# Another order of work in the mixed layers of a small float32 network: units of the projection, heads, linear attention and output projection

## The chip, the core and the metric

One core of a Trainium2 chip runs the whole network in one launch. Its engines are TensorE (PE, matrix products), VectorE (DVE), ScalarE (ACT), GpSimd (POOL) and the queue SP, which issues the loads. Each engine takes its instructions strictly in the order in which the program gives them, and waits at semaphores that the others raise. The metric is the device time of one execution in microseconds (us), lower is better.

## What is computed

The input is 256 tokens of width 1024. A first block has two layers of feed-forward (width 2816), a mixer, and feed-forward again; a second block has four layers of another kind. The change is in the mixer of the first block (called a mixed layer here), of which the core of the reference is:

```python
proj = h @ mix_w_in[l]
a_q, a_k, a_v, b_u, c_q, c_k, c_v, c_r, c_g = jnp.split(proj, splits, axis=-1)
qa = _rope(_rmsnorm(_split_heads(a_q, ATT_HEADS), q_norm[l]), cos, sin)
ka = _rope(_rmsnorm(_split_heads(a_k, ATT_HEADS), k_norm[l]), cos, sin)
o_a = _merge_heads(_moba_attention(qa, ka, va))
o_b = _conformer_conv(b_u, conv_w[l], conv_b[l], conv_norm_g[l], conv_norm_b[l])
log_decay = jax.nn.log_sigmoid(c_g @ gla_gate_w[l] + gla_gate_b[l]) / GLA_TAU
o_c = _gla(...)
o_c = _merge_heads(_rmsnorm(o_c, gla_out_norm[l])) * jax.nn.silu(c_r)
mixed = jnp.concatenate([o_a, o_b, o_c], axis=-1) @ mix_w_out[l]
x = x + gt2[:, None, :] * mixed
```

With 256 tokens the attention is one causal block: eight heads of width 64. The convolution is depthwise, 31 taps on 256 channels, then a layer norm over groups of 64 channels and swish. The linear attention has four heads of width 64. The second block's layers are differential attention (twice), HGRN (once) and a gated unit (once), each followed by cross-attention and feed-forward. All is float32 in value.

## The kernel before

**Products of split weights.** Every weight arrives as float32 in `raw`, four slots of 1 MB (a *unit*: 1024 rows by 256 columns). ACT rounds it into `whi` (line 782), DVE subtracts to get `wlo` (line 1204), and PE takes three products (high by high, high by low, low by high) into a PSUM bank. `ahead(pos)` (split_ahead) on ACT and on DVE makes these splits for units up to three ahead of `pos`, and each split waits until PE has used up the unit that held the slot before. A unit is 48 products of 256 columns, two accumulation halves of 24 products, each of which shows as two or one records in the trace.

**The mixed layer, `mix1`.** Each engine's list is written out by hand. PE (lines 2204 to 2291): thirteen units in the order c_r, c_g (half a unit), c_k, c_q, conv_a, conv_g, mq, mq, mk, mk, c_v, mv, mv; among them a small gate product, four sums of squares for the head norms (`group_sum`, line 2183) and four rope products (line 2300). Then, when all units are done, a loop of eleven steps: `scores` of head j (lines 2266 and 2267, into bank 4 or 0 by turns), transposes of head j-2 (`turn_probs`, line 1956, bank 6), `values` of head j-3 (`over_tokens`, lines 2202 and 2203, bank 7 or 3), the linear attention's three levels (lines 2243 and 2247) at j below 3, its token product at j = 4, and two sums for the convolution's norm (lines 2286 and 2290). DVE (to line 1751) copies c_v and mv out, does the 62 tap instructions (lines 1579 and 1582) in blocks of 4, 10 and 12 between the splits, the ropes, and for each head mask, maxima, reciprocal and the two scalings of the probabilities (lines 1706 to 1717). ACT copies the other units out, does roots (lines 938 and 940), the exponentials (line 945), the copies of the transposes (line 992) and the high parts of the results (line 998).

**The output projection, `outp`** (line 2505 on), is four units of the same kind (line 2518), each over eight tiles k of the mixed result; unit 0 waits tile by tile for the result's low part: tiles 0 to 3 are attention, 4 and 5 convolution, 6 and 7 linear attention. DVE adds each unit to x (line 1474), and the norm of the next feed-forward begins with squares on ACT, a sum on PE (line 2091), a logarithm and an exponential on ACT (lines 841 and 843), and then eight high and low parts (lines 856 and 1369) that release the first unit of the feed-forward tile by tile.

**HGRN** has its own list: `HGRN_ORDER`, five whole units, then levels of its recurrence between halves of units (`level`, line 2197 on PE; `up`, lines 1527 to 1540, and `keep_level`, lines 1557 and 1561 on DVE). `half(u, src, m)` is one accumulation half of a unit; the differential layer uses it to put each head between two halves.

## Time and profile before

| | |
|---|---|
| Time, median of 3 runs | 2830.16 us (2827.55 to 2834.45) |
| The profiled execution's own time | 2832.67 us |
| Its span, first to last instruction | 2830.8 us |
| Mean granted TensorE clock | 0.972 |
| PE busy in the span | 2699.1 us (95%) |
| DVE / ACT busy | 1870.0 us (66%) / 1343.5 us (47%) |
| First mixed layer, first unit to last product of the output projection | 286.3 to 446.1 us |
| Second mixed layer | 847.9 to 1008.9 us |

The times are of one profiled execution. A busy share is an average over stages. Where lines of PE stand as x2, two records were merged; matmuls are pipelined, so that the start of the next instruction less the start of this one is what an instruction costs in a full queue, and the printed duration is longer. PEclk is the granted clock as a share of 2.4 GHz: 0.50 is 1.2 GHz.

### The profile page before, as it was taken

What the parts mean: (1) busy time and instruction counts of PE and PEld (TensorE: products, weight loads), DVE (VectorE), ACT (ScalarE), POOL (GpSimd) and SP (SyncE); (2) the same over time, 40 slices, a digit from 0 to 9 for tenths busy, and PEclk for the clock granted to TensorE, in tenths of its full rate; (3) what the DMA queues carried; (4) which work ended last, traced back from release to release, by engine and by line L of the source; (5) the groups of instructions that cost most, each with busy time, mean ns of one, the idle gap of its engine ahead of it and who ended that gap; (6) DMA issues with size and microseconds to landing.
All of it is one profiled execution on the core that took longest, in us unless ns stands there. A gap on an engine that the chain in (4) does not pass through costs nothing.

```text
span 2830.8 us, 52843 instructions
## 1 busy us (share of the span) xinstructions
PE 2699.1 (95%) x22247; PEld 2615.9 (92%) x22247; DVE 1870.0 (66%) x2575; ACT 1343.5 (47%) x1578; POOL 3.5 (0%) x7
## 2 busy tenths in 40 slices
PE   6799979999999799999999999999999999999998
PEld 5799859999999499999999999999999999999998
DVE  5788776887877655576565666656565555775564
ACT  3334634435445354455544535544455544655443
POOL 0000000000000000000000000000000000000000
PEclk8899979999999699999999999999999999999999
DMA  8988505997985046654355643535665365643553
GB/s 234 310 291 273 179 30 187 300 294 263 299 282 164 30 150 200 205 189 162 101 199 179 210 147 105 164 135 196 220 194 179 105 208 198 209 145 118 179 192 105
DMA packets 458801, 533.05 MB, mean 188 GB/s; under 512 B 9880, under 2 KB 435082, under 8 KB 458634
## 3 DMA queue, kind: packets, MB, share of 16 engines
q1 hardware_dynamic: 457340, 530.11, 57.4%
q8 instruction: 112, 1.84, 0.3%
q10 hardware_dynamic: 1293, 0.65, 0.1%
q14 instruction: 56, 0.45, 0.0%
HBM read 528.10 MB, written 2.62 MB: 187 GB/s over the span
## 4 chain that ended last, share of the span: by engine, by line
PE 84%; DVE 8%; ACT 3%; issue 2%; DMA 2%; SPq 1%; ACTq 0%; DVEq 0%
PE ps L2134 15%; PE ps L1965 12%; PE ps L1966 12%; PE ps L1967 12%; PE ps L1983 10%; PE ps L2518 8%; DVE wlo L1204 2%; DMA work<-in_ada_w 2%; PE ps L2168 2%; DVE work L1582 1%; PE ps L2327 1%; PE ps L2329 1%; PE ps L2328 1%; PE ps L2091 1%; DVE work L1308 1%
## 5 line engine op out<-in xcount | busy, mean ns | idle before, releaser
L1204 DVE TENSOR_TENSOR wlo<-raw,whi 128x2048 fp32r<-128x2048 f32 (+1 forms) x514 | 975.8, 1918 | 411.5 <-ACT whi L782 411.3
L782 ACT ACTIVATE whi<-raw 128x2048 fp32r<-128x2048 f32 (+1 forms) x514 | 827.7, 1616 | 442.3 <-PE ps L1967 181.6
L1965 PE MATMUL ps<-hhi,whi 128*128 128x256 f32 x1600 | 451.9, 282 | 16.0 <-issue 14.2
L1966 PE MATMUL ps<-hlo,whi 128*128 128x256 f32 x1600 | 445.5, 278 | 0.0
L1967 PE MATMUL ps<-hhi,wlo 128*128 128x256 f32 x1600 | 445.1, 278 | 0.0
L1965 PE MATMUL ps<-parts_f,whi 128*128 128x256 f32 x1344 | 372.9, 277 | 8.0 <-issue 8.0
L1966 PE MATMUL ps<-parts_f,whi 128*128 128x256 f32 x1344 | 371.8, 277 | 0.0
L1967 PE MATMUL ps<-parts_f,wlo 128*128 128x256 f32 x1344 | 371.5, 276 | 0.0
L2134 PE MATMUL ps<-ghi,whi 128*128 128x256 f32 x1280 | 355.5, 278 | 7.9 <-DVE wlo L1204 7.9
L2134 PE MATMUL ps<-glo,whi 128*128 128x256 f32 x1280 | 355.5, 278 | 0.0
L2134 PE MATMUL ps<-ghi,wlo 128*128 128x256 f32 x1280 | 355.2, 278 | 0.0
L1965 PEld LDWEIGHTS ps<-hhi,whi 128*128 128x128 f32 x1600 | 303.7, 190 | 20.3 <-issue 20.3
L1966 PEld LDWEIGHTS ps<-hlo,whi 128*128 128x128 f32 x1600 | 303.8, 190 | 0.7 <-issue 0.7
L1967 PEld LDWEIGHTS ps<-hhi,wlo 128*128 128x128 f32 x1600 | 303.4, 190 | 0.0
L1965 PEld LDWEIGHTS ps<-parts_f,whi 128*128 128x128 f32 x1344 | 252.3, 188 | 9.5 <-issue 9.4
L1966 PEld LDWEIGHTS ps<-parts_f,whi 128*128 128x128 f32 x1344 | 252.3, 188 | 0.1
L1967 PEld LDWEIGHTS ps<-parts_f,wlo 128*128 128x128 f32 x1344 | 252.3, 188 | 0.0
L2134 PEld LDWEIGHTS ps<-ghi,whi 128*128 128x128 f32 x1280 | 241.5, 189 | 8.6 <-issue 8.6
L2134 PEld LDWEIGHTS ps<-glo,whi 128*128 128x128 f32 x1280 | 241.5, 189 | 0.0
L2134 PEld LDWEIGHTS ps<-ghi,wlo 128*128 128x128 f32 x1280 | 241.4, 189 | 0.0
L1308 DVE SCALAR_TENSOR_TENSOR work<-work,silu_c 128x256 f32<-128x256 f32 x490 | 196.9, 477 | 0.0
L1983 PE MATMUL ps<-hhi,whi 128*128 128x256 f32 x880 | 177.9, 284 | 16.3 <-DVE hlo L1369 16.3
(299 smaller groups left out, 4818.2 us busy)
## 6 DMA issues: line engine op xcount, KB each, us to landing
raw<-in_ffn_w_in SPq DMA_DIRECT2D x88, 1024.0 KB, 10.5
raw<-in_ffn_w_gu SPq DMA_DIRECT2D x88, 1024.0 KB, 5.1
work<-in_ada_w SPq DMA_DIRECT2D x72, 1024.0 KB, 8.9
raw<-in_ffn_w_out SPq DMA_DIRECT2D x88, 512.0 KB, 5.9
raw<-in_ffn_w_down SPq DMA_DIRECT2D x88, 512.0 KB, 5.5
raw<-in_ca_w_kv SPq DMA_DIRECT2D x32, 1024.0 KB, 5.6
raw<-in_mix_w_in SPq DMA_DIRECT2D x24, 1024.0 KB, 6.2
raw<-in_da_w_in SPq DMA_DIRECT2D x24, 1024.0 KB, 5.5
```

What stands on the lines that cost most here:

```text
L782: f(whi[:, s, 0:size], raw[:, s, 0:size], ACT.Copy).then_inc(hi_done[s], 1)
L1204: tt(wlo[:, s, 0:size], raw[:, s, 0:size], whi[:, s, 0:size].bitcast(F32), ALU.subtract).then_inc(lo_done[s], 1)
L1308: m = stt(acc, w, silu_c[:, k:k + 1], acc, ALU.mult, ALU.add)
L1582: m = stt(conv_acc[:, t, :], h, w, conv_acc[:, t, :], ALU.mult, ALU.add)
L1965: mm(dst, wh, xh, start=first, stop=False)
L1966: mm(dst, wh, xl, start=False, stop=False)
L1967: return mm(dst, wl, xh, start=False, stop=last)
L1983: o = mm(ps[:, slot, 256 * m:256 * m + 256], w[:, k, P * m:P * m + P], x_[:, k, :], start=k == 0 and i == 0 and m == 0, stop=k == KT - 1 a ...
L2091: o = mm(ps[:, st.bank, 0:S], ones, norm_x[:, k, :], start=k == 0, stop=k == KT - 1)
L2134: o = mm(dst, a_, b_[:, t, :], start=first and t == 0 and i == 0 and m % 2 == 0, stop=False, skip_group_check=True)
L2168: o = mm(dst, a_, b_[:, t, :], start=False, stop=t == 1 and i == 2 and m % 2 == 1, skip_group_check=True)
L2518: o = mm(ps[:, bank, 256 * m:256 * m + 256], w[:, k, P * m:P * m + P], x_[:, k, :], start=k == 0 and i == 0 and m == 0, stop=k == KT - 1 a ...
```

## The change

In the mixed layer the thirteen units come in the order of `MIX_ORDER`: convolution's gate and input first, the gate of linear attention, then queries and keys by turns, and the rest; their PSUM banks go round over three. From the fourth unit on PE takes each unit in halves, and head norms, ropes, scores, transposes, values and the levels of linear attention stand between halves. Scores now use bank 4 alone, values bank 7 alone, sums bank 5, ropes bank 3. Masking, maxima and reciprocal stay on DVE; the scaling of probabilities, and the copying out of mv and c_v, move to ACT. DVE's taps lie in blocks of 2 to 10 over the whole layer, 15 or more at its end. Two merged predicated copies take the place of four in the linear attention's `keep`. The output projection is taken in parts (`out(n, *ks)`), by the tiles that are ready: 0 and 1 of its units among the last heads, then 2, 3, 6 and 7, and last 4 and 5; the order 0, 1, 2, 3, 6, 7, 4, 5 is in `ORDER`. Its inputs lie in `fhi`/`flo` in place of `hhi`/`hlo`; `outp` on PE does nothing after a mixed layer, and during it ACT and DVE call `ahead` for two of its units only, DVE after the last addition to x. In the HGRN layer `hf` comes ahead of `hq`, and DVE's `ahead(us[LEAD].pos)` moves from before the first level's `keep` to after it.

```diff
                       ("dk", 1, 2), ("dv", 2, 2), ("dq", 0, 3), ("dk", 1, 3), ("dv", 2, 3))
+        MIX_ORDER = (("conv_g", 1792, 0, 256), ("conv_a", 1536, 0, 256), ("c_g", 2960, 0, P), ("mq", 0, 0, 256),
+                     ("mk", 512, 0, 256), ("mq", 0, 1, 256), ("mk", 512, 1, 256), ("mv", 1024, 0, 256),
+                     ("c_k", 2304, 0, 256), ("c_q", 2048, 0, 256), ("mv", 1024, 1, 256), ("c_v", 2560, 0, 256),
+                     ("c_r", 2816, 0, 256))
         LEAD = 5
-        HGRN_ORDER = (("hq", 0, 0), ("hq", 0, 1), ("hf", 1, 0), ("hf", 1, 1), ("hq", 0, 2),
+        HGRN_ORDER = (("hf", 1, 0), ("hf", 1, 1), ("hq", 0, 0), ("hq", 0, 1), ("hq", 0, 2),
                       ("hq", 0, 3), ("hf", 1, 2), ("hf", 1, 3), ("hv", 2, 0), ("hv", 2, 1), ("hv", 2, 2),
                       ("hv", 2, 3), ("hgate", 3, 0), ("hgate", 3, 1), ("hgate", 3, 2), ("hxv", 4, 0),
...
-        def out_project(w, mod=None):
-            units = plan.columns(w, 0, 4, "out")
+        def out_project(w, mod=None, banks=None):
+            units = [plan.column(w, 0, "out", n, banks[n] if banks else plan.slot) for n in range(4)]
...
-            units += plan.columns(w, 1024, 2, "mv", token_major=True)
+            units = [plan.column(w, c0, name, i, n % 3, token_major=name in ("mv", "c_v"), cols=cols, bank=name not in ("mq", "mk"))
+                     for n, (name, c0, i, cols) in enumerate(MIX_ORDER)]
...
+                                masked=take("masked", 8), pairs=take("pairs", 4), rope=take("rope", 4),
+                                reads=list(plan.reads)))
...
+            ready = out_project(a["mix_w_out"][l], mod=(l, 1), banks=(1, 2, 0, 3))
+            mixed.out = stages[-1]
...
+                def probabilities(j):
+                    s, r = m_s[:, j % 2, :], stat[:, j % 2]
+                    act.wait_ge(q["scaled"], st.heads + j + 1)
+                    f(s[:, 0:P], s[:, 0:P], ACT.Copy, scale=r[:, 8:9])
+                    f(s[:, P:384], s[:, P:384], ACT.Copy, scale=r[:, 9:10]).then_inc(q["probs"], 1)
...
+                tt(conv_h[:, :, CONV_K - 1:], rows2(ps[:, us[1].b, :]), conv_sig, ALU.mult).then_inc(read[us[1].b], 1)
+                dve.wait_ge(*bank_read(us[1]))
+                taps_on(4)
+                ahead(us[2].pos)
+                taps_on(4)
+                gate_least()
+                ahead(us[3].pos)
+                taps_on(2)
+                gate_sums()
+                ahead(us[4].pos)
+                taps_on(3)
+                normed(0)
+                taps_on(6)
+                ahead(us[5].pos)
+                normed(1)
+                rope(0)
+                taps_on(4)
+                ahead(us[6].pos)
+                normed(2)
+                rope(1)
+                ahead(us[7].pos)
+                maxima(0)
+                normed(3)
+                rope(2)
+                inverse(0)
+                maxima(1)
+                ahead(us[8].pos)
+                inverse(1)
+                maxima(2)
                 rope(3)
-                causal = const("causal")
-                for j in range(8 + 3):
-                    if j < 8:
...
+                maxima(4)
+                queries_in()
+                inverse(4)
+                ahead(us[10].pos)
+                maxima(5)
+                taps_on(2)
+                inverse(5)
+                keep(0)
+                low(1)
+                ahead(us[11].pos)
+                maxima(6)
+                taps_on(2)
+                inverse(6)
+                keep(1)
+                far()
+                maxima(7)
+                taps_on(2)
+                inverse(7)
+                ahead(us[12].pos)
+                keep(2)
+                low(2)
+                taps_on(10)
+                ahead(st.out.units[0].pos)
+                taps_on(8)
+                low(3)
+                taps_on(2 * CONV_K)
...
+                tt(rows2(m_t[:, 0, :]), rows2(m_t[:, 0, :]), c_r, ALU.mult).then_inc(q["gla_out"], 1)
+                dve.wait_ge(q["conv_mm"], 2 * l + 1)
+                dve.wait_ge(q["taps_v"], base + 2 * CONV_K)
+                stt(conv_acc, rows2(ps[:, 4, :]), -1.0 / HD, conv_acc, ALU.mult, ALU.add).then_inc(q["conv_v"], 1)
                 dve.wait_ge(q["gla_hi"], l + 1)
                 dve.wait_ge(q["gla_out"], l + 1)
-                tt(hlo[:, 6:8, :], rows2(m_t[:, 0, :]), hhi[:, 6:8, :].bitcast(F32), ALU.subtract)\
+                tt(flo[:, 6:8, :], rows2(m_t[:, 0, :]), fhi[:, 6:8, :].bitcast(F32), ALU.subtract)\
...
@@ -1854,7 +1949,7 @@
                         for m in range(H_DONE[g - 1], H_DONE[g]):
                             evict(us[m + 1])
                             ahead(us[m + 2].pos)
-                    else:
+                    if g == 1:
                         ahead(us[LEAD].pos)
                     if g == LEVELS + 5:
                         normed(0)
...
+                def values(h):
+                    pair = h // 2
+                    pe.wait_ge(q["turned"], st.heads + h + 1)
+                    pe.wait_ge(*bank_read(us[7 if h < 4 else 10]))
+                    if h == 0:
+                        pe.wait_ge(q["gate_v"], 2 * l + 1)
+                        pe.wait_ge(q["gate_s"], 3 * l + 1)
+                    if st.pairs + pair > 0:
+                        pe.wait_ge(q["values_lo"], st.pairs + pair)
+                    over_tokens(ps[HD * (h % 2):HD * (h % 2) + HD, 7, 0:S], mv, slice(HD * h, HD * h + HD),
+                                m_pt[:, h % 2, :]).then_inc(q["values_mm"], 1)
...
+                def conv_sum(n):
+                    if n == 0:
                         pe.wait_ge(q["taps_v"], 2 * CONV_K * (l + 1))
...
+                        pe.wait_ge(q["masked"], st.masked + 8)
+                    else:
...
+                def out(n, *ks):
+                    u = outs[n]
...
+                    if ks[0] == ORDER[0]:
+                        weights(u)
+                        if u.read > 0:
+                            pe.wait_ge(read[u.b], u.read)
+                    th, tl = tiles(u.slot)
+                    bank = out_bank(st.out, n)
+                    for k in ks:
+                        pe.wait_ge(*mixer_tile(st.out, k))
+                        for i, (w, x_) in enumerate(((th, fhi), (th, flo), (tl, fhi))):
+                            for m in range(2):
+                                o = mm(ps[:, bank, 256 * m:256 * m + 256], w[:, k, P * m:P * m + P], x_[:, k, :],
+                                       start=k == ORDER[0] and i == 0 and m == 0,
+                                       stop=k == ORDER[-1] and i == 2 and m == 1, skip_group_check=True)
+                    if ks[-1] == ORDER[-1]:
+                        o.then_inc(used[u.slot], 1)
+                for n in range(3):
+                    unit(us[n], "h", st.h)
+                half(us[3], "h", 0)
+                gates()
+                half(us[3], "h", 1)
+                half(us[4], "h", 0)
+                head_sum(0)
+                half(us[4], "h", 1)
+                half(us[5], "h", 0)
+                head_sum(1)
...
+                half(us[5], "h", 1)
+                pe.wait_ge(q["gn_out"], st.gn + 1)
+                half(us[6], "h", 0)
+                head_sum(2)
+                rope(1)
+                half(us[6], "h", 1)
+                pe.wait_ge(q["gn_out"], st.gn + 2)
+                half(us[7], "h", 0)
+                head_sum(3)
+                rope(2)
+                scores(0)
+                half(us[7], "h", 1)
+                scores(1)
+                pe.wait_ge(q["gn_out"], st.gn + 3)
+                half(us[8], "h", 0)
+                rope(3)
+                turn_head(0)
+                scores(2)
+                half(us[8], "h", 1)
+                turn_head(1)
+                values(0)
+                pe.wait_ge(q["gn_out"], st.gn + 4)
+                half(us[9], "h", 0)
+                turn_head(2)
+                values(1)
+                scores(3)
+                half(us[9], "h", 1)
+                scores(4)
+                half(us[10], "h", 0)
+                values(2)
+                turn_head(3)
+                scores(5)
+                half(us[10], "h", 1)
+                turn_head(4)
+                values(3)
+                gla_level(0)
+                half(us[11], "h", 0)
+                turn_head(5)
+                scores(6)
+                half(us[11], "h", 1)
+                values(4)
+                gla_level(1)
+                half(us[12], "h", 0)
+                values(5)
+                turn_head(6)
+                scores(7)
+                half(us[12], "h", 1)
+                gla_level(2)
+                out(0, 0, 1)
+                values(6)
+                turn_head(7)
+                out(1, 0, 1)
+                gla_tokens()
+                out(2, 0, 1)
+                values(7)
+                out(0, 2)
+                out(1, 2)
+                group_sum(st.gn + 4, 3, m_sq, block)
+                out(2, 2)
+                conv_sum(0)
+                out(0, 3)
+                out(1, 3)
+                out(2, 3)
+                out(3, 0, 1)
+                conv_sum(1)
+                out(3, 2, 3)
+                for n in range(4):
+                    out(n, 6, 7)
+                for n in range(4):
+                    out(n, 4, 5)
...
             def outp(st):
+                if st.mixer.kind == "mix1":
+                    return
```

## Rows read from the trace of the kernel before

**Rows 1.** The page, section 1: busy time of each engine over the whole span
```profile
PE 2699.1 (95%) x22247; PEld 2615.9 (92%) x22247; DVE 1870.0 (66%) x2575; ACT 1343.5 (47%) x1578; POOL 3.5 (0%) x7
```

**Rows 2.** Busy time by stretch (columns in its first line), first mixed layer
```profile
core 0: us, PE busy (x) PEld busy (x) DVE busy (x) ACT busy (x) POOL busy (x), PEclk, DMA share, GB/s
286.30:376.00 89.70, 79.36 (x622) 73.82 (x623) 72.80 (x108) 47.04 (x47) 1.39 (x1) 0.97 0.49 155
376.00:420.00 44.00, 37.69 (x150) 22.72 (x149) 26.08 (x83) 16.34 (x50) 0.00 (x0) 0.60 0.00 1
420.00:446.10 26.10, 24.12 (x195) 23.86 (x194) 13.21 (x17) 13.10 (x14) 0.00 (x0) 0.93 0.34 116
```

**Rows 3.** The same view: a differential layer, HGRN's levels, after a norm
```profile
1209.40:1341.80 132.40, 131.33 (x1090) 125.15 (x1089) 91.95 (x123) 76.84 (x128) 0.00 (x0) 1.00 0.52 167
...
1650.00:1700.00 50.00, 45.39 (x377) 44.84 (x375) 35.15 (x60) 15.81 (x14) 0.00 (x0) 0.97 0.33 106
...
452.00:458.00 6.00, 5.68 (x35) 5.71 (x36) 5.41 (x14) 4.02 (x8) 0.00 (x0) 0.72 0.00 0
```

**Rows 4.** The chain that ended last, in time: start, us, what
```profile
286.34 6.32 PE ps L1983 x48
...
446.05 3.47 PE ps L2091 x16
...
452.32 7.35 PE ps L1983 x48
...
847.93 7.40 PE ps L1983 x48
...
1008.88 3.47 PE ps L2091 x16
...
1353.83 21.80 PE ps L1983 x192
```

**Rows 5.** Timeline of PE, small matmuls: start, us, engine, line, operation, shape
```profile
399.81 0.55 PE L1956 MATMUL ps<-con,work 128*128 128x128 f32 x3
...
400.29 0.65 PE L2202 MATMUL ps<-work 128*64 128x256 f32 x2
...
401.09 0.48 PE L2266 MATMUL ps<-work 64*128 64x128 f32 x2
...
407.51 1.91 PE L2183 MATMUL ps<-work,con 128*128 128x512 f32 x2
...
409.35 0.79 PE L2266 MATMUL ps<-work 64*128 64x128 f32 x2
```

**Rows 6.** Timeline of DVE: taps, weight split, rope, one head's maxima
```profile
340.80 4.83 DVE L1582 SCALAR_TENSOR_TENSOR work<-work,taps 128x256 f32<-128x256 f32 x12
...
345.54 2.29 DVE L1204 TENSOR_TENSOR wlo<-raw,whi 128x2048 fp32r<-128x2048 f32 x1
...
348.41 0.68 DVE L1594 TENSOR_TENSOR work<-ps,cs 128x512 f32<-128x512 f32 x1
...
350.33 4.83 DVE L1582 SCALAR_TENSOR_TENSOR work<-work,taps 128x256 f32<-128x256 f32 x12
...
387.07 0.55 DVE L1706 TENSOR_TENSOR work<-ps,con 128x384 f32<-128x384 f32 x1
...
388.18 0.15 DVE L1518 RECIPROCAL stat<-stat 128x2 f32<-128x2 f32 x1
```

**Rows 7.** Timeline of ACT: a table load; the last weight split before a norm; ACT free after it
```profile
319.29 1.28 ACT L820 ACT_TABLE_LOAD   x1
...
435.26 1.92 ACT L782 ACTIVATE whi<-raw 128x2048 fp32r<-128x2048 f32 x1 [3.52 <-PE ps L2518]
...
457.09 1.28 ACT L873 ACT_TABLE_LOAD   x1
```

**Rows 8.** Timeline at HGRN's first two levels: DVE, then PE
```profile
1640.85 2.29 DVE L1204 TENSOR_TENSOR wlo<-raw,whi 128x2048 fp32r<-128x2048 f32 x1 [2.71 <-ACT whi L782]
...
1644.33 2.05 PE L2197 MATMUL ps<-work 128*128 128x128 f32 x16 [1.48 <-DVE work L1527]
```

486 lines of the change are left out of this document (238 added, 248 removed).

## Prediction

> **What bounds the kernel now.** I read the page first, then busy time by stretch, then the timeline of each engine in the stretch that stood out. The page says PE is busy for 95% of the span [rows 1], which looks like a kernel with nothing to gain from order. That is an average. By stretch [rows 2], the first mixed layer has three parts: 89.7 us of units (clock 0.97), 44.0 us in which the heads, linear attention and convolution's norm run alone, and 26.1 us of output projection. In the middle part PE counts as busy for 37.7 us, but at a granted clock of 0.60, so that its work is 37.7 x 0.60 = 22.6 us at full clock; DVE is busy for 26.1 us of the 44 and ACT for 16.3. Nobody is full: the engines hand each other one head at a time. What the layer costs from its first unit to the norm's sum is 446.05 - 286.34 = 159.7 us, and for the second layer 1008.88 - 847.93 = 161.0 us [rows 4]. The differential layer, in which heads already stand between halves of units, is the model of the other state: PE busy 131.3 of 132.4 us, clock 1.00 [rows 3].
>
> **PE's floor in the new order.** The products stay the same; only the time at which they run changes. A unit costs 21.80 / 4 = 5.45 us when the queue is full [rows 4]. Units: 12.5 x 5.45 = 68.1 us, plus 0.9 because the first is released tile by tile (6.32) [rows 4]. Output projection: 4 x 5.45 = 21.8. Small products: a sum or rope over 512 columns takes 409.35 - 407.51 = 1.84 at half clock, 0.92 at full [rows 5]; four sums, four ropes and the gate product (512 columns too) that now lie among the units are 9 x 0.92 = 8.3, and with the 22.6 from above 30.9. Floor: 68.1 + 0.9 + 21.8 + 30.9 = 121.7 us a layer. Of the 30.9 the heads take most: transposes 400.29 - 399.81 = 0.48, values 401.09 - 400.29 = 0.80, scores (as many columns) the same, so 8 x 2.08 = 16.6 [rows 5].
>
> **DVE in the new order.** It is busy for 72.8 + 26.1 + 13.2 = 112.1 us of the layer [rows 2]. Sixteen scalings and three copies go to ACT (an estimate of 7 us: 0.3 each for the scalings, 0.64 for a copy, a third of the rope's three passes over as many elements), about 105 us stay, less than PE's floor, so DVE isn't the bound by its sum; what matters is where its work lies. Its prices from start to start: twelve taps 345.54 - 340.80 = 4.74, so 0.395 each; a rope's three passes 350.33 - 348.41 = 1.92; a weight split 2.2; mask and maxima 388.18 - 387.07 = 1.1 [rows 6]. Followed down the three lists, DVE keeps ahead of PE through the early units, since each unit gives it 5.45 us against a split of 2.2 and 1 to 3 us of taps or ropes. The weak place is the end. PE issues `scores(7)` after 11.5 units' worth plus a half, 65.4, the 0.9, and 30.9 - 6.8 of small products (6.8 for two values 1.6, one transpose 0.5, level and tokens some 1.9, three sums 2.8): 90.4, with a little handshake 91. From there DVE has, without a gap: mask and maxima 1.1, two taps 0.8, the reciprocal 0.3, a split 2.2, `keep` 0.9, `low` 0.35, ten taps 3.95, a split 2.2, eight taps 3.2, `low` 0.35, and the last 62 - 47 = 15 taps 5.9. That is 21.3, so the taps end at 112.3. `conv_sum(0)` waits for them in PE's queue, and PE reaches it at about 91 + 2.7 (half unit) + 5.0 (small) + 6.1 (nine tiles of output, 0.68 each) = 105. PE therefore idles for 7 us there, and all the remaining output parts stand behind that wait although their tiles may be ready. After it: 0.9 + three tiles 2.0 + two 1.4 + sum 0.9 + two 1.4 + eight 5.4 + eight 5.4 = 17.5 (rounded from tiles of 0.68), end at 129.8. The convolution's own chain from 113.2 (mean 0.7, square 0.6, PE's sum at its turn ending 117.5, root 1.3, gain 0.8, table 1.3 [rows 7] and swish 0.9, high 0.6, low 0.7) is ready at 123.1, and PE needs it at 124.3: hidden by only 1.2 us, and one for one on the path beyond that.
>
> **Clock.** After the norm's wait PE starts at half clock, 0.72 over six us [rows 3], and its first unit takes 7.35 where 6.32 was seen [rows 4]. I charge the 7 us wait at `conv_sum(0)` the same 1.0. First layer 131, second layer 132 (it starts at 7.40 [rows 4]). Saved: 159.7 - 131 = 28.7 and 161.0 - 132 = 29.0, together 57.7.
>
> **What is lost behind the layer.** Now the second unit of the following feed-forward is rounded by ACT at 435.26, while the output projection runs [rows 7]. In the change `outp` calls `ahead` for two units only, so this split moves behind the norm's last high part: ACT is free at 457.09 [rows 7], rounds in 1.9, DVE subtracts in 2.2, ready at 461.3. PE is through with the first unit at 452.32 + 7.35 = 459.7 [rows 4]. That is 1.6 us of idle a layer, 3.2 in all; queued behind are all products of the feed-forward. The first unit's `wlo`, which DVE does after its last addition to x, lies beside square, sum and root (the first product comes 6.3 us after the sum starts [rows 4]) and costs nothing. Loads cost nothing: the DMA share is 0.49, 0.00 and 0.34 in the three stretches [rows 2], and the same 17 MB in 131 us is about 130 GB/s.
>
> **HGRN.** DVE waits 2.71 us for ACT's rounding before it can do the second level's factor, and PE idles 1.48 for it [rows 8]. The moved `ahead` takes this wait out of the way; the work that comes next in DVE's list has slack of a half unit. With `hf` first, its DVE part is done before `hq` is there, which PE isn't waiting for today. I take 1.5; bounds 0 and 3.5 (the wait could return at the next level, or a second one of the same sort could go too).
>
> **Other edits.** Merged `keep` copies the same elements in half as many instructions, within 0.5 us. The half unit c_g moves from second to third place, so that DVE splits a whole unit before the norm's scaling: 1 us more, inside its wait for the root; if that cover were gone, 1 us a layer. ACT does about 5 us more scaling and 2 of copies; it is busy 76 of 160 us [rows 2].
>
> **Sum.** 57.7 - 3.2 + 1.5 = 56.0. Against the profiled execution (2832.67 us, span 2830.8) this gives 2776.7. The median of the runs is 2.5 below that execution: 2774.
>
> **Rivals.** *Floor* (0.10): DVE is faster than I lay out or PE slower early, so that the taps are done when PE comes; 122.7 and 123.7 a layer, with the upper HGRN value 37.0 + 37.3 + 3.5 - 0 = 77.8, so 2752. For it: the differential layer idles only 1.1 us [rows 3]. Against: that layer has no taps.
> *Handshakes* (0.12): a head's round trip is scores 0.8, maxima 1.1, exponentials 1, scaling 0.9, transposes 0.5, copy 0.5, values 0.8, and with a DVE split of 2.2 and an ACT split of 1.9 in between nearly 10 us, against some 8 us between heads with only two in flight and now one bank for scores. If each of eight costs PE 1.5 more, the layer takes 143 and the time is 2798. Against: in the differential layer the same trip hides.
> *Slower, by the clock* (0.05): the change puts a wait into nearly every half unit. Now the long units run clear of heads at 0.97 while only the small products suffer at 0.60 [rows 2]; if the small waits pull the clock down among the units too, the last 4.5 units, the 4 of output (8.5 x 5.45 = 46) and 15 us of small products run at 1.2 GHz: 192 a layer, 2893 in all. It decides where more than 29 us of a layer's work falls to half clock. Against it: from 1650 to 1700 PE has such waits (busy 45.4 of 50) and keeps 0.97 [rows 3]. The Trainium skill has a rule for this case, speaking against the change: "TensorE: Matmul & The Clock Gate", section "A second HAM failure mode: psum-queue depth-cycling", says that many short idle gaps between groups of matmuls can make the clock oscillate. By that rule the time would be this rival's; the row of the HGRN levels bears it out hardly at all.
> *No overlap* (0.03): the chain of taps, norm and swish plus late heads eats what the interleaving gives, 2826 to 2835; DVE would have to idle 50 us a layer, which no stretch of its lists suggests.
>
> **Chances and range.** Forecast 0.70 (2757 to 2792: tail idle 3 to 12 us a layer, waits of heads up to 5). A measurement of this kernel tells about 0.3% from no change. Faster by more than that 0.92 (forecast, floor, handshakes), within it 0.03, slower 0.05. The range, 2755 to 2799, takes in handshakes and nearly the floor.
>
> **What would show it.** PE idle at the product that answers to line 2286 (sum over taps), released by DVE's taps: 5 to 9 us; clock 0.95 or more from the first head to there; a layer of 129 to 134 us; the feed-forward's second unit waiting 1 to 2 us for `wlo`; no 1.48 us wait at HGRN's second level. The prediction is wrong if transposes or values wait over 1 us for most heads, if the clock falls between units, or if ACT's splits come late because exponentials stand in front of them.

## The result, and the profile after

The changed kernel takes 2790.17 us (median of 4 runs, 2786.83 to 2792.43) against 2830.52 us before (median of 4, 2827.55 to 2834.45): a ratio of 0.9856, 95% interval 0.9839 to 0.9873. The forecast was 2774 us, range 2755 to 2799. The profiled execution took 2786.83 us with a span of 2785.0 us, where the kernel before had 2832.67 and 2830.8. It is these 45.8 us of span that the account below divides up; the medians are 40.4 us apart, since the profiled execution before lies 2.1 us above its median and the one after 3.3 us below.

Busy time of the engines over the whole span, after, and then the first mixed layer by stretch (start and end, length, busy us and instructions of each engine, granted clock, DMA share, GB/s):

```profile
PE 2675.4 (96%) x22247; PEld 2602.8 (93%) x22247; DVE 1858.3 (67%) x2525; ACT 1356.7 (49%) x1615; POOL 3.5 (0%) x7
```

```profile
284.30:300.00 15.70, 15.67 (x125) 15.70 (x126) 14.15 (x28) 11.70 (x13) 0.00 (x0) 0.90 0.58 179
300.00:384.00 84.00, 84.00 (x626) 72.32 (x625) 63.19 (x103) 51.25 (x94) 1.38 (x1) 1.00 0.42 137
384.00:402.00 18.00, 11.61 (x78) 8.82 (x76) 17.79 (x40) 6.91 (x9) 0.00 (x0) 0.94 0.00 1
402.00:419.60 17.60, 17.60 (x142) 16.63 (x140) 5.58 (x11) 10.51 (x13) 0.00 (x0) 0.96 0.00 1
```

The 44 us at clock 0.60 [rows 2] are gone. PE is busy for all of the 84 us in which heads stand between halves of units, at full clock. One hole is left, 384 to 402, and in it DVE is full (17.79 of 18.00). What PE waited for in this layer (for what, us in total, times, longest):

```profile
PE ps L2398 <- DVE work L1637: 5.8, 1, 5.8
PE ps L2078 <- DVE hlo L1422: 2.8, 1, 2.8
PE ps L2297 <- DVE parts_f L1757: 0.6, 1, 0.6
```

L2398 is `conv_sum`, L1637 a tap of the convolution; the 2.8 us are the norm's, and were there before. The chain of waits in the same layer, in order of time (start, us, what):

```profile
284.33 12.63 PE ps L2078 x96
...
379.22 0.57 DVE work L1746
...
394.50 5.21 DVE work L1637 x14
...
400.49 2.08 PE ps L2398 x2
402.56 3.92 PE ps L2415 x30
...
407.34 12.28 PE ps L2415 x108
419.62 3.67 PE ps L2186 x16
```

From the first product to the norm's sum the layer takes 419.62 - 284.33 = 135.3 us, and the second 961.86 - 825.62 = 136.2 us, where they took 159.7 and 161.0 [rows 4]. The reader should see the last taps end at 400.4 and `conv_sum` start at once.

**Where the 45.8 us are.** I took the start of every norm's sum in both traces and subtracted stretch by stretch. Mixed layers, from their first product: 24.4 + 24.8 = 49.2 gained. The feed-forward behind each layer, sum to sum, grew: 198.5 to 202.0 and 194.0 to 197.4, so 6.9 lost. The stretch with HGRN's levels went from 194.7 to 192.9, 1.9 gained. All before the first mixed layer is 2.0 shorter, though no instruction there changed, and 0.4 is lost in small amounts elsewhere. That is scatter: over all runs below, the first mixed layer begins anywhere between 282.7 and 287.1. 49.2 - 6.9 + 1.9 + 2.0 - 0.4 = 45.8.

The loss behind the layer shows in the second layer's feed-forward. Timeline of ACT, DVE and PE at its start (start, us, engine, line, operation, shape, idle before and for whom):

```profile
973.00 1.90 ACT L788 ACTIVATE whi<-raw 128x2048 fp32r<-128x2048 f32 x1
...
974.93 2.29 DVE L1257 TENSOR_TENSOR wlo<-raw,whi 128x2048 fp32r<-128x2048 f32 x1 [1.32 <-ACT whi L788]
...
977.33 0.55 PE L2060 MATMUL ps<-hhi,whi 128*128 128x256 f32 x1 [2.66 <-issue]
977.67 0.42 PE L2061 MATMUL ps<-hlo,whi 128*128 128x256 f32 x1
```

ACT rounds the second weight unit after the norm's last high part, DVE subtracts, and PE starts 0.1 us after DVE ends. The row says "issue", but DVE's end at 977.22 shows what was waited for. Behind the idle time the products come to stand 0.21 apart (0.34 for the first) instead of 0.11: half clock.

The first layer's feed-forward has something more. It streams the modulation weights of the layers to come, and here ACT's waits for its weights' loads, from the norm's sum on, are 8.6 us before (first row) and 40.6 us after (second row):

```profile
ACT whi L782 <- DMA raw<-in_ffn_w_in: 8.6, 9, 1.5
```

```profile
ACT whi L788 <- DMA raw<-in_ffn_w_in: 40.6, 19, 6.6
```

The stretches say why. Before, the last 12 us of the output projection, the 15 us behind them, and the rest of the feed-forward:

```profile
434.10:446.10 12.00, 12.00 (x107) 11.98 (x106) 4.06 (x6) 5.00 (x5) 0.00 (x0) 1.00 0.73 251
446.10:461.10 15.00, 12.18 (x79) 11.47 (x78) 7.53 (x19) 8.16 (x14) 0.00 (x0) 0.89 0.18 58
461.10:644.60 183.50, 183.26 (x1606) 183.06 (x1605) 149.41 (x235) 79.03 (x69) 0.00 (x0) 1.00 0.89 288
```

And after, the same three, with the third cut in two:

```profile
407.60:419.60 12.00, 12.00 (x107) 11.87 (x106) 4.20 (x9) 9.14 (x11) 0.00 (x0) 1.00 0.00 1
419.60:434.60 15.00, 11.04 (x65) 10.11 (x64) 11.67 (x21) 10.14 (x17) 0.00 (x0) 0.89 0.21 70
434.60:449.60 15.00, 14.28 (x123) 14.15 (x124) 8.52 (x7) 6.69 (x6) 0.00 (x0) 1.00 0.95 319
449.60:621.60 172.00, 171.41 (x1496) 171.12 (x1495) 140.99 (x228) 72.37 (x62) 0.00 (x0) 1.00 0.91 293
```

Before, the loads ran at 251 GB/s while the output projection was still on (251 x 12 = 3.0 MB); after, at 1 GB/s. A load can start when DVE has subtracted the unit that lay in its raw slot. Before, DVE does that between the additions to x, and the next load goes out 11.8 us ahead of the norm's sum (first row: the queue, start, us, loads). After, DVE comes to it behind the last addition, and the load goes out 3.3 us behind the sum, as soon as this subtraction ends (second and third row):

```profile
434.14 5.82 SPq L664 DMA_DIRECT2D raw<-in_ffn_w_in  x2
...
420.45 2.28 DVE L1257 TENSOR_TENSOR wlo<-raw,whi 128x2048 fp32r<-128x2048 f32 x1
422.81 12.62 SPq L670 DMA_DIRECT2D raw<-in_ffn_w_in  x2
```

Two things in the change could make the load late: in the parts by ready tiles all four units are used up together at the end, and ACT and DVE call `ahead` for two units only, DVE after the last addition. The run with the output projection whole (below) parts them. The feed-forward then asks for some 290 GB/s to its end and doesn't catch up.

### The profile page after: what moved, and what is told of

Read it like the earlier page. It is cut to its first block, busy times and chain, and to the rows that moved or that the text cites. A ratio compares the mean times of both kernels' runs of the same rounds, so it can differ in the third digit from the quotient of the medians.

```text
span 2785.0 us, 52844 instructions
## 1 busy us (share of the span) xinstructions
PE 2675.4 (96%) x22247; PEld 2602.8 (93%) x22247; DVE 1858.3 (67%) x2525; ACT 1356.7 (49%) x1615; POOL 3.5 (0%) x7
## 4 chain that ended last, share of the span: by engine, by line
PE 88%; DVE 5%; issue 2%; DMA 2%; ACT 2%; SPq 1%; ACTq 0%; DVEq 0%
PE ps L2229 15%; PE ps L2060 13%; PE ps L2061 13%; PE ps L2062 13%; PE ps L2078 8%; PE ps L2720 6%; PE ps L2527 2%; PE ps L2529 2%; PE ps L2528 2%; DMA work<-in_ada_w 2%; PE ps L2263 2%; PE ps L2186 1%; PE ps L2415 1%; DVE work L1361 1%; PE ps L2051 1%
## 5 line engine op out<-in xcount | busy, mean ns | idle before, releaser
L2060 PE MATMUL ps<-hhi,whi 128*128 128x256 f32 x1824 | 518.5, 284 | 21.7 <-issue 19.7
L2061 PE MATMUL ps<-hlo,whi 128*128 128x256 f32 x1824 | 508.5, 279 | 0.0
L2062 PE MATMUL ps<-hhi,wlo 128*128 128x256 f32 x1824 | 507.6, 278 | 0.0
L2060 PEld LDWEIGHTS ps<-hhi,whi 128*128 128x128 f32 x1824 | 346.4, 190 | 31.7 <-issue 31.5
L2061 PEld LDWEIGHTS ps<-hlo,whi 128*128 128x128 f32 x1824 | 346.3, 190 | 2.2 <-issue 2.2
L2062 PEld LDWEIGHTS ps<-hhi,wlo 128*128 128x128 f32 x1824 | 346.1, 190 | 0.0
L2078 PE MATMUL ps<-hhi,whi 128*128 128x256 f32 x656 | 132.3, 284 | 16.2 <-DVE hlo L1422 16.2
```

What stands on the lines that cost most here:

```text
L2060: mm(dst, wh, xh, start=first, stop=False)
L2061: mm(dst, wh, xl, start=False, stop=False)
L2062: return mm(dst, wl, xh, start=False, stop=last)
L2078: o = mm(ps[:, slot, 256 * m:256 * m + 256], w[:, k, P * m:P * m + P], x_[:, k, :], start=k == 0 and i == 0 and m == 0, stop=k == KT - 1 a ...
```

## The experiments

The first four, the dummies behind units and the fewer bytes are single runs; the others are timed in three or five rounds. "Mixed layer" is always from the first product to the norm's sum, "sum to sum" the feed-forward behind it. The kernel before, timed beside the first four, took 2827.9 us.

**HGRN alone.** The kernel before with nothing but HGRN's two edits:

```
-        HGRN_ORDER = (("hq", 0, 0), ("hq", 0, 1), ("hf", 1, 0), ("hf", 1, 1), ("hq", 0, 2),
+        HGRN_ORDER = (("hf", 1, 0), ("hf", 1, 1), ("hq", 0, 0), ("hq", 0, 1), ("hq", 0, 2),
...
-                    else:
+                    if g == 1:
                         ahead(us[LEAD].pos)
```

> The kernel before with the two HGRN edits alone (hf ahead of hq, the look-ahead split after the first keep). Theory: they are worth the 2 us by which the HGRN layer is shorter in the changed kernel (450.0 against 452.1 us from the feed-forward's last products before it to those after it), and nothing else moves: 450.0 here too, a span some 2 us shorter than 2830.8, within the scatter of single executions. Rival: the 2 us came from the earlier layers' other timing (clock or loads); then this layer stays at 452.1.

Measured: 2828.3 us, span 2826.5; mixed layer 159.9. A single time can't show 2 us; the trace can. PE's waits from the sum before HGRN to the sum after it, first before, then with the edits:

```profile
PE ps L2197 <- DVE work L1527: 2.9, 2, 1.5
```

```profile
PE ps L2197 <- DVE work L1527: 1.4, 1, 1.4
```

One wait of 1.5 is gone, the others stay (five for L1537, 4.7 us in both). The stretch is 194.7 before and 191.2 here, but it lies between 191.2 and 193.4 in all kernels with these edits: 1.3 to 3.5 gained, of which 1.5 is shown by the wait.

**Is it the clock?** The kernel before with 108 products more a layer in the stretch of heads, twelve behind each of nine head steps, whose results nobody reads:

```
+                    if j not in (6, 7):
+                        if j == 8:
+                            pe.wait_ge(q["conv_s"], 4 * l + 2)
+                        for _ in range(12):
+                            mm(ps[:, 2 if j in (4, 5) else 5, 0:256], ghi[:, 0, 0:P], ghi[:, 1, :], start=True, stop=True)
```

> The kernel before, with twelve dummy products of 256 columns added to nine of the eleven steps of the loop over heads in each mixed layer (their results are never read). They are 108 x 0.1135 = 12.3 us of extra PE work a layer at full clock. Theory 'clock': in the 44.0 us stretch the heads' work is 22.6 us at full clock, so 15 us of it are lost to the half clock; kept busy, PE stays at 0.9 or more and the stretch, with 12 us more work, takes 40 to 46 us, no longer than before. Theory 'handshakes': the stretch is long because engines wait for each other and the clock only follows; then the dummies come on top and it takes 50 us or more even where the clock is near 1.00.

Measured: 2832.5 us, mixed layer 160.1. The stretch of heads of the first layer (the second has 0.85 too):

```profile
376.00:420.00 44.00, 39.13 (x228) 29.24 (x229) 25.91 (x82) 15.56 (x48) 0.00 (x0) 0.85 0.00 1
```

The clock rose from 0.60 [rows 2] to 0.85, and the layer took as long as before. That is the number of the theory 'clock' (40 to 46 us); the 50 us of 'handshakes' didn't come. But it doesn't price the clock either: PE's work, taken as busy time by granted clock, grew from 37.7 x 0.60 = 22.6 to 39.13 x 0.85 = 33.3 us, so the dummies took the place that the clock gave back, and no run shows the stretch at a high clock without them. The change removed the low clock and the handing over together; how the gain divides between the two stays open.

**Whole units.** The changed kernel, each unit whole and the small products behind it:

```
-                half(us[3], "h", 0)
+                unit(us[3], "h", None)
...
-                half(us[3], "h", 1)
-                half(us[4], "h", 0)
+                unit(us[4], "h", None)
...
```

> The changed kernel, but PE takes each of the ten units whole, and the small products that stood between its halves come behind it, in the same sequence. Fewer changes between unit products and small ones: 10 in place of 19. In the changed kernel 456 unit products between halves took 55.9 us, 4.2 more than at 0.1135 each. Theory 'change of kind costs': half of the 4.2 us comes back on PE, but heads come in lumps, two scores or transposes at a time, and PE waits for DVE and ACT; with scores in one bank the two together leave a mixed layer of 137 to 145 us against 135.3. Rival 'halves don't matter': 133 to 136.

Measured: 2794.8 us; mixed layers 140.0 and 139.5, so 4.7 and 3.3 more than in halves. PE's waits in the first one:

```profile
PE ps L2398 <- DVE work L1637: 4.2, 1, 4.2
PE ps L2297 <- DVE parts_f L1757: 3.8, 1, 3.8
...
PE ps L2338 <- DVE work L1746: 1.5, 2, 0.7
```

A head's round trip fits less well between whole units (L2297 3.8, L2338 1.5), and part of that is given back at the taps (4.2 for 5.8). Halving is worth 3 to 5 us a layer, not more. The expectation's other half didn't come. The unit products behind the first three units took 4.2 and 4.6 us more than at 0.1134 each in the two layers of the changed kernel, where they follow small products in 15 places; here, with 9 such places, they took 3.9 and 3.7 us more. Not half came back, but 0.3 and 0.9.

**Output projection whole, at the end.**

```
-                out(0, 0, 1)
...
-                out(1, 0, 1)
...
-                    out(n, 6, 7)
-                for n in range(4):
-                    out(n, 4, 5)
+                    out(n, *ORDER)
```

> The changed kernel with the output projection taken out of the list of heads and run whole at the end, unit by unit over all eight tiles. Theory: the convolution's chain after the last tap (ready some 11 us after the taps' end in the changed kernel) now has only the first unit's six tiles (4.1 us) in front of it, and 12 us of output parts no longer lie beside the last heads: each mixed layer 8 to 12 us longer than 135.3, so 143 to 147. Rival: the output parts only fill time in which PE would have waited anyway for the taps; then the layer grows by less than 4 us.

Measured: 2805.5 us; mixed layers 144.9 and 144.7, so 9.6 and 8.5 more. From 383 to 405:

```profile
383.00:405.00 22.00, 10.84 (x37) 5.66 (x38) 18.49 (x40) 7.86 (x11) 0.00 (x0) 0.62 0.00 1
```

```profile
PE ps L2398 <- DVE work L1637: 9.3, 1, 9.3
```

Without the parts PE stands before the taps for 9.3 us, then through the convolution's norm and swish, at clock 0.62. The parts fill this tail. They are worth 9 us a layer.

This run also tells what the loads of the feed-forward wait for. The units are used up one by one again, the first at 411.25, where DVE adds it to x; yet DVE's next subtraction and the load behind it stand where the changed list puts them, behind the last addition:

```profile
411.25 0.88 DVE L1528 SCALAR_TENSOR_TENSOR x<-ps,mods,x 128x256 f32<-128x256 f32 x2 [1.78 <-PE ps L2415]
...
428.38 2.28 DVE L1257 TENSOR_TENSOR wlo<-raw,whi 128x2048 fp32r<-128x2048 f32 x1
430.73 12.41 SPq L670 DMA_DIRECT2D raw<-in_ffn_w_in  x2
```

The load goes out 3.3 us behind the norm's sum, as in the changed kernel, and the feed-forward takes 205.9 us from sum to sum. So the place of the splits in the lists of ACT and DVE is enough to make the loads late, and the joint use of the four units isn't needed for it. Whether the parts would hold the loads up with the splits moved forward was not run.

**The same kernel again**, as the neighbour of the next three.

> The changed kernel itself, once more, as the base for the three beside it. Both theories: ratio 0.984 to 0.987 to the kernel before, mixed layers 135 to 136 us, PE waiting 5.8 us in each for the last tap.

Measured: 2792.27 us, ratio 0.9864 (0.9846 to 0.9882); mixed layers 135.1 and 136.2, and sum to sum 205.7 and 197.4. The first of these was 202.0 in the other execution of the same kernel: a stretch limited by loads scatters by 4 us, the second hardly at all.

**Taps earlier.** DVE does 33 taps more among the heads, so that fewer are left for the tail:

```
                 rope(1)
+                taps_on(4)
...
                 rope(2)
+                taps_on(5)
...
                 keys_in()
+                taps_on(9)
...
                 inverse(5)
+                taps_on(4)
...
                 inverse(6)
+                taps_on(5)
                 keep(1)
                 far()
+                taps_on(6)
```

> The changed kernel with the convolution's taps moved forward into the places where DVE idles between heads (4, 5, 9, 4, 5 and 6 taps at six places), so that none is left for the end. Theory 'late taps': the wait of 5.8 us at the sum over the taps goes, with the half clock behind it about 6 to 7 us a layer, 12 to 14 in all: about 2777 against 2790. Rival 'heads need DVE': the taps now stand in front of maxima and reciprocals, PE waits for scores and probabilities in place of taps; then less than 6 us in all.

Measured: 2776.37 us, ratio 0.9807 (0.9786 to 0.9828); mixed layers 129.3 and 128.4, 5.8 and 7.8 less than its neighbour. All that PE waits for from 360 to the norm's sum, and the stretch where the taps' wait was:

```profile
PE ps L2303 <- DVE parts_f L1757: 0.6, 1, 0.6
```

```profile
385.00:400.00 15.00, 14.37 (x111) 11.85 (x107) 7.05 (x9) 8.48 (x12) 0.00 (x0) 1.00 0.00 1
```

The wait at `conv_sum` is gone and nothing took its place. The late taps were the bound at the end of the layer, and 128 to 129 us is what PE's own list takes (127.7 to 129.6 in the kernels below that keep these taps).

**The second weight unit earlier.** ACT rounds it between the norm's squares and its root:

```
-                if st.early or st.defer is not None:
+                if st.early or st.defer is not None or st.gain[0] == "ffn2_norm":
                     ahead(st.pos)
```

> The changed kernel with one split moved: ACT rounds the feed-forward's second unit between the norm's squares and its root, where it waits 2.1 us for PE's sum, and no longer after the norm's last high part. Theory 'late split': PE's wait of 2.7 us for this unit's low part (2.7 in the second layer) shrinks by 1.3 to 2.0 us a layer, as DVE's subtraction stays behind the last low part; 3 to 4 us in all, seen between the norm's sum and the feed-forward's first output products (33.9 us in the second layer). Rival 'clock': what is lost there is the clock's fall after the norm; then that stretch stays within 0.5 us.

Measured: 2785.52 us, ratio 0.9848 (0.983 to 0.9867); sum to sum 204.1 and 194.6. ACT in the first layer's norm:

```profile
418.86 2.33 ACT L840 ACTIVATE work<-x 128x512 f32<-128x512 f32 x4
421.10 1.90 ACT L788 ACTIVATE whi<-raw 128x2048 fp32r<-128x2048 f32 x1
423.31 0.47 ACT L847 ACTIVATE rstd<-ps,con 128x256 f32<-128x256 f32 x1 [0.31 <-PE ps L2186]
```

The split fits in front of the root, which isn't delayed. In the second layer the feed-forward is back at 194.6, against 194.0 before the change and 197.4 after it: the late split costs 2.8 of the 3.4. In the first layer 1.6 came back, within the scatter of its loads. The median is 6.7 us below its neighbour's, more than the trace explains, but the intervals of the two ratios overlap.

**Another cut of the halves.** By k instead of by column, so that a unit's products run in the order of a whole one:

```
+                if by_k:
+                    for k in range(4 * m, 4 * m + 4):
+                        for i, (w, x_) in enumerate(((th, xh), (th, xl), (tl, xh))):
+                            for n in range(2):
...
-                half(us[3], "h", 0)
+                half(us[3], "h", 0, True)
```

> The changed kernel with halves cut the other way: the first half takes the tiles 0 to 3 of the sum for both column groups, the second 4 to 7, in the order of products that whole units have. Same products, same places. Theory 'order within a half': unit products between small ones cost 0.1226 us each because of their order and the restart of each group; at 0.1135 each layer gains up to 4 us, 8 in all. Rival 'change of kind': the extra is paid at each change between unit products and small ones whatever the order; then the time stays within 2 us of the changed kernel's.

Measured: 2790.84 us, ratio 0.9863 (0.9846 to 0.988); mixed layers 135.2 and 136.0, as without it. The unit products behind the first three units take 4.1 and 4.3 us more than at 0.1134 each, against 4.2 and 4.6 without the edit. The order of products within a unit is not what makes units dearer among small products.

**What a small product costs the unit behind it.** The kernel with both edits (below), and dummy products without any wait in the looped steps of three feed-forwards:

```
+                        if not isinstance(n, int):
+                            w, x_, cols = (th[:, 0, 0:P], hi[:, 0, :], 256) if st.i == 5 else (block, ident, P)
+                            for _ in range({3: 2, 4: 4 * m, 5: 2}.get(st.i, 0)):
+                                o = mm(ps[:, O0, 0:cols], w, x_, start=True, stop=True)
```

> The disputed cost by itself, in the kernel with both edits: dummy products without any wait in the eight looped steps of three feed-forwards. In the fourth (second layer's second), two fp32 products of 128 columns behind each half unit, 64 in 32 places; in the fifth, four behind each whole unit, 64 in 16 places; in the sixth, two fp32r products of 256 columns behind each half unit, 64 in 32 places. Theory (a change between fp32 and fp32r products costs time in the unit that follows): the half units behind them take 0.1 to 0.3 us more than 2.72, so the fourth grows by 64 x 0.23 = 14.7 plus 3 to 9 us, the fifth by 14.7 plus half of that, the sixth by 64 x 0.1135 = 7.3 and nothing more. Rival (what costs is the wait at the small product or at the half unit, not the kind): no wait, no cost, the fourth and the fifth grow by the same 14.7 us, and half units stay at 2.72.

Measured, sum to sum against the same stretch without dummies: fourth 210.2 for 194.7, +15.6; fifth 200.3 for 183.1, +17.1; sixth 190.4 for 183.1, +7.3. PE in the fourth, around one pair of dummies:

```profile
1023.96 0.61 PE L2227 MATMUL ps<-con 128*128 128x128 f32 x4
1024.32 0.37 PE L2066 MATMUL ps<-hhi,whi 128*128 128x256 f32 x1
1024.53 0.28 PE L2067 MATMUL ps<-hlo,whi 128*128 128x256 f32 x1
...
1027.17 0.61 PE L2227 MATMUL ps<-con 128*128 128x128 f32 x4
```

The half unit takes 1027.17 - 1024.32 = 2.85 us; the 24 halves between two pairs all take 2.84 or 2.85. In the sixth, behind fp32r dummies, all 32 take 2.72. On the rows the first theory is right: the half unit is longer, though PE never stood still. But most of these 0.125 us are a shift between neighbours, and no cost. From start to start, the first product behind the dummies takes 0.20 instead of 0.11. The dummies in front of it show as two records each, 0.11 apart, but the last one takes only 0.03, so that a pair comes to 0.363 and four to 0.807, some 0.09 to 0.10 less than their records at 0.1134. Taken together, a place with a pair costs 0.363 + 0.125 = 0.49 us (x 32 = 15.6, as measured), 0.03 more than four records; that is nearer to the rival.

Behind four dummies there is more. A unit takes 5.58 instead of 5.44 and the output products 5.79, which is 0.14 and 0.35 more, of each of which 0.10 is the shift. In all a place with four costs 17.1 / 16 = 1.07 us, 0.16 more than eight records. Neither theory had both totals: 14.7 plus 3 to 9 and plus half of that for the first, 14.7 twice for the rival. The run has no waits, so it says nothing of what a wait would add; and its fp32 and fp32r dummies differ in columns (128 and 256) and operands as well as in kind.

**Both edits together**, taps earlier and the second unit's rounding earlier.

> The kernel after with both edits: DVE's taps moved forward among the heads, and ACT's rounding of the feed-forward's second unit between the norm's squares and its root. If the two terms are independent they add up: mixed layers 129.3 and 128.4 us as with the taps alone, and about 2 us a layer less from the norm's sum to the feed-forward's first output product, together 2771 to 2774 us. Rival: in the first layer the following feed-forward is bound by its loads, so that an earlier split there is given back, and only the second layer keeps its 2 us: 2774 to 2776.

Measured: 2771.44 us (2770.05 to 2771.95, 5 runs), ratio 0.9788 (0.9775 to 0.9801); mixed layers 127.9 and 128.3, feed-forwards 202.0 and 194.7. It is the fastest version with a reason for each of its parts, and it beats both kernels: 19 us under the changed one. The two terms add up: against the changed kernel's 0.9864, the taps take 0.57% and the rounding 0.16% off the ratio, and both together 0.76%.

**Loads sent earlier.** In addition, SP sends the first four loads of modulation weights in front of those that wait for a slot:

```
+                        if st.i == 1:
+                            sp.wait_ge(q["norm_sq"], 4 * (st.h + 1))
+                            for n in range(per[0] + per[1]):
+                                ada(u + n)
                         stream(st.pos + 2 + 4)
```

> As the kernel with both edits, and SP sends the first four loads of modulation weights of the first layer's second feed-forward as soon as the norm's squares are done, ahead of the loads that wait for a raw slot. Theory (loads start late): in the kernel after, the DMA engines stand at a share of 0.00 to 0.21 up to 434 us and then carry about 295 GB/s to the end of that feed-forward, and ACT waits 40.6 us there for loads; sent 12 us earlier, the same bytes take the feed-forward from about 205 us back to 199 or less, ACT's wait for loads to 10 us or less, and the total to 5 to 6 us below its neighbour. Rival (rate alone): the loads are limited by the rate whatever the start, or the fifth weight unit, now sent behind four others, comes late itself: length 204 to 208, total the same or up to 3 us more.

Measured: 2770.20 us, ratio 0.9784 (0.9771 to 0.9797), no difference from its neighbour; sum to sum 204.6. From the norm's sum, two times 18 us and the rest, and ACT's wait for loads:

```profile
414.30:432.30 18.00, 14.96 (x98) 14.02 (x98) 11.96 (x21) 10.18 (x16) 0.00 (x0) 0.91 0.92 290
432.30:450.30 18.00, 13.98 (x109) 13.81 (x108) 12.00 (x17) 8.64 (x7) 0.00 (x0) 0.91 0.84 288
450.30:618.90 168.60, 168.60 (x1480) 168.60 (x1479) 137.97 (x218) 70.69 (x62) 0.00 (x0) 1.00 0.85 274
```

```profile
ACT whi L792 <- DMA raw<-in_ffn_w_in: 10.7, 6, 5.0
```

```profile
438.20 0.55 PE L2070 MATMUL ps<-hhi,whi 128*128 128x256 f32 x1 [4.02 <-issue]
```

Both theories have half of it. With the transfers earlier, 290 GB/s in the first 18 us instead of 107 in the neighbour, ACT's waits fall from 41.2 to 10.7 us and PE is full from 450 on, so the late start is the cause of the waits later on. But the weights of the feed-forward's second step now stand behind four other loads, and PE waits 4.0 us for them at 438. Two loads instead of four in front might keep the gain; that was not run.

**Fewer bytes.** With both edits, the twenty modulation loads of that feed-forward carry an eighth of their bytes.

> As the kernel with both edits, but the twenty loads of modulation weights in the first layer's second feed-forward carry an eighth of their bytes each (the modulation they give is left out of the result; the additions and products on them all run). If loads are what holds this feed-forward: ACT's wait for loads of weights falls from about 40 us to under 5, its length from about 205 to 196 to 199 us. If its excess over the kernel before (198.5 us) comes from anything else, such as the late split or the order of DVE's work, it stays at 203 to 206.

Measured: 2765.9 us; sum to sum 199.1 against 202.0 in its neighbour and 202.0 to 206.0 in the other kernels with the late splits; the kernel before has 198.5, and 199.1 and 199.4 in the two experiments built on it. The share of the DMA engines from 448 on is 0.59 instead of about 0.9:

```profile
448.10:611.10 163.00, 163.00 (x1431) 163.00 (x1431) 135.43 (x212) 67.04 (x60) 0.00 (x0) 1.00 0.59 193
```

```profile
ACT whi L789 <- DMA raw<-in_ffn_w_in: 0.9, 1, 0.9
```

With the bytes gone, the waits and the extra 3 to 7 us are gone. The loads hold this feed-forward in the changed kernel.

## Why the prediction was right, and where it was off

The sign, the mechanism and the place of the remaining wait came as forecast; the time was 16 us (0.6%) too low. Step by step:

**The clock and the stretch of heads: right.** The forecast had the layer without any half clock stretch, and PE full until `conv_sum(0)`. It is full for 84 us at 1.00. The rival that feared the clock named a rule of the Trainium skill ("TensorE: Matmul & The Clock Gate", section "A second HAM failure mode: psum-queue depth-cycling"), by which many short gaps make the clock oscillate. The trace doesn't put it to the test: small products stand between nearly all half units, but PE is busy for all 84 us, so the short idle gaps didn't come, and the granted clock of that stretch is 1.00.

**The floor of PE: mis-sized, and this is most of the error.** The prediction had 121.7 us, and 1.0 for the clock. With the taps moved away, so that PE waits 0.6 us, the layers take 127.9 to 129.3; and the changed kernel less its waits is 135.3 - 5.8 - 0.6 = 128.9. So the term is 5 to 7 us too low, per layer. Summed over the trace of the first layer, each product from its start to the next one's and without the waits:

| us | forecast | measured |
|---|---|---|
| units | 68.1 + 0.9 + 1.0 = 70.0 | 73.9 |
| small products | 30.9 | 29.8 |
| output projection | 21.8 | 25.1 |
| waits | 131 less the above: 8.3 | 6.4 |

The step "Units: 12.5 x 5.45" took the price of a unit in a long undisturbed row [rows 4] for one among small products, and so did "4 x 5.45" for the parts of the output. In the trace of after, 456 products of units between 303 and 382 take 55.9 us and not 51.8: 4.1 more, in 15 places behind small products. 2.5 of it is in the first product of each place, which takes 0.22 in twelve of them and 0.52 behind the three sums and ropes over 512 columns. The run with dummies shows that such a first product mostly takes over what the small one in front of it lacks, and the small products are indeed 1.1 shorter than forecast. So units and small products have to be taken together: 103.7 for 100.9, 2.8 too low. The other 1.6 is spread over the products behind, 0.113 to 0.123 on average in the 15 places. What slows them isn't shown. It isn't the order within a half, and it hardly fell with the number of places when units were taken whole.

The output's parts are 3.3 over their price. In the kernel with the taps moved they take 24.1, so 2.3 belong to parts that stand among small products, and 1.0 to the lower clock behind the wait. The trace of before could have warned. In the differential layer, where heads stand between halves of units, PE's timeline has this half unit:

```profile
1244.35 0.39 PE L1965 MATMUL ps<-hhi,whi 128*128 128x256 f32 x1
...
1247.31 0.49 PE L1956 MATMUL ps<-con,work 128*128 128x128 f32 x3
```

It takes 2.96 us, and the unit price would give 2.72.

**The tail of taps: right, and shifted.** Forecast: `scores(7)` at 91, then 21.3 us of DVE work, end at 112.3, PE waiting 7. Measured: DVE begins that work at 379.22 - 284.33 = 94.9 and ends at 400.43, 21.2 later, at 116.1; PE waits 5.8 (5.7 in the second layer). The sum over DVE's list was right to 0.1 us; its start was late by what PE's units took more. The wait is within the 5 to 9 that the prediction named.

**Behind the wait.** 17.5 + 1.0 forecast, 419.62 - 400.43 = 19.2 measured. The convolution's chain stayed hidden: L2415 follows L2398 without a wait, and 12.28 us of output parts run to the sum.

**Saved per layer**: 24.4 and 24.8 instead of 28.7 and 29.0, 8.5 us less in the two together: about 6 a layer by the floor, less the 2 that the waits were shorter than forecast.

**The late split: right in kind, half the size.** Forecast 1.6 a layer, "ready at 461.3", so 15.25 us after the sum's start. It came 977.22 - 961.86 = 15.4 after. But PE was done earlier than the row of before said: its first unit took 6.2 us (968.33 to 974.5) and not 7.35. The wait is 2.66, and the half clock behind it takes some 1.4 more over thirteen products. The split earlier gives 2.8 back in the second layer.

**"Loads cost nothing": wrong.** The step looked at the bytes inside the mixed layer, where they do cost nothing. It didn't ask when DVE's list, with its splits moved behind the last addition to x, frees the raw slots for the next stage's loads, though the step on the late split had that move in it. This loss is in the first layer's feed-forward alone, since there the loads already take a share of 0.89 before the change: together with the split it is 3.5 in the two profiled executions, 7.2 in the other one of the changed kernel, and its waits for loads go from 8.6 to 40.6 us. The profile of before shows what was at stake in two rows, 251 GB/s in the output projection and 288 in the feed-forward.

**HGRN: right.** 1.5 forecast, with one wait of 1.5 gone; 1.9 measured in the stretch.

**The rivals.** *Floor* didn't come: DVE's tail was there, and without it the layer still takes 128 to 129 us and not 122.7; *handshakes* neither, PE waiting 0.6 us for heads in the whole layer; but the 2790 us lie nearer to the second's 2798 than to the forecast, by another cause. *Slower, by the clock* and *no overlap* are refuted by the stretches above.

In terms of the sum: 57.7 became 49.2, the 3.2 behind the layers 6.9, HGRN's 1.5 became 1.9, so 56.0 became 44.2; with 1.6 of scatter it is the 45.8 of the spans. That is 10 of the 16 us. The other 6 lie between executions: the forecast took the median 2.5 below the profiled execution, as before the change, and after it the median is 3.3 above.

## What to carry to other kernels

Where small work is moved between large units, price the large units and the small ones together, from a place where they already stand side by side, and not each from its own long rows: here that is 5 to 7 us of a layer of 135. When a change takes splits or other work out of a stage, ask which buffers that work freed and which transfers stand behind them, in the next stage too: the feed-forward with its DMA engines at 0.9 didn't make up a late start. And a list of one engine's work, priced row by row, gave the length of its tail to 0.1 us; where that tail ends last, moving a part of it forward gave back its full length (waits of 5.8 and 5.7 us gone, layers 5.8 and 7.8 shorter, 2792.3 to 2776.4 us).

## What the runs showed of the hardware

A half unit of 24 fp32r products takes 2.72 us behind fp32r products and 2.84 or 2.85 behind two fp32 ones, with no wait between: its first product takes 0.20 instead of 0.11. Most of that is missing in front of it, where the last fp32 record takes 0.03 instead of 0.11. A pair of fp32 products of 128 columns in front of a half unit lengthened the stretch by 0.49 us (15.6 / 32), a pair of fp32r products of 256 columns by 0.23 (7.3 / 32), and four fp32 ones by 1.07 (17.1 / 16).

Dummy products raised the granted clock of the stretch of heads from 0.60 to 0.85; PE's work there at full clock grew from 22.6 to 33.3 us, and the layer took 160.1 us against 159.7.

The same kernel's feed-forward at a DMA share of 0.9 took 202.0 us in one execution and 205.7 in another, while the second layer's, with a share of 0.60, took 197.4 both times.
